# A mixer round's attention scores made in two halves, with the next round's first projection between them

## The reference

```python
h = rms_norm(x, g_mix[l])
z = h @ w_in[l]                                   # 1024 -> 6 x 512
u, gb, gc, q, k, v = jnp.split(z, splits, axis=-1)
y_conv = gb * short_conv(gc * u, conv_w[l])       # causal, width 3
q = rms_norm(q per head, g_q[l]) * (HEAD_DIM ** -0.5)
k = rms_norm(k per head, g_k[l])                  # 8 heads of 64
y_attn = dilated_mixture(q, k, v)                 # three dilated windows, mixed by exp(lse)
mix = concat(rms_norm(y_conv), rms_norm(y_attn))
x = x + mix @ w_out[l]
...                                               # gated feed-forward, then the second block
```

## Time and profile before

| what | value |
|---|---|
| median of 3 runs | 996.63 us |
| the profiled execution's own time | 998.33 us |
| its span from first to last instruction | 996.7 us |
| TensorE busy | 975.9 us (98%) |
| VectorE busy | 679.9 us (68%) |
| ScalarE busy | 415.0 us (42%) |
| mean granted TensorE clock, of full | 0.995 |
| rounds 0 to 3 of the mixer | about 39 to 190 us of the span |
| 512 KB weight load, median from issue to landing | 3.7 us |

### The profile page before, as it was taken

The page is one execution under the profiler, slowest core; times in us unless marked ns, Lnnn a source line. Parts: engine busy times, 40 slices in busy tenths (PEclk is TensorE's granted clock), DMA queues, the critical chain, the costliest instruction groups (busy, mean ns, idle before and its releaser), DMA issues.

```text
span 996.7 us, 14071 instructions
## 1 busy us (share of the span) xinstructions
PE 975.9 (98%) x4648; PEld 784.3 (79%) x4648; DVE 679.9 (68%) x1218; ACT 415.0 (42%) x671; POOL 171.7 (17%) x298
## 2 busy tenths in 40 slices
PE   6999999999999999999999999999999999989997
PEld 6876777677888888888888876888888887757886
DVE  6585786687676666655346668498978766865656
ACT  5455454634332323333221236945552326652343
POOL 3010101100000000197200000835760000000000
PEclk9999999999999999999999999999999999999999
DMA  6336757232562332334423223332243334542332
GB/s 216 92 92 201 203 165 197 55 97 85 170 188 85 105 104 86 91 109 136 145 90 105 85 75 109 100 85 69 64 106 88 101 100 89 149 116 69 107 89 85
DMA packets 146228, 112.22 MB, mean 113 GB/s; under 512 B 5100, under 2 KB 136428, under 8 KB 146188
## 3 DMA queue, kind: packets, MB, share of 16 engines
q1 hardware_dynamic: 138768, 85.83, 29.3%
q0 software_dynamic: 7184, 25.84, 9.5%
q10 hardware_dynamic: 236, 0.06, 0.0%
HBM read 99.65 MB, written 4.20 MB: 104 GB/s over the span
## 4 chain that ended last, share of the span: by engine, by line
PE 93%; DMA 2%; ACT 2%; DVE 2%; issue 0%; SPq 0%; DVEq 0%
PE bank L623 20%; PE bank L624 19%; PE bank L625 19%; PE bank L884 4%; PE bank L882 4%; PE bank L883 4%; PE bank L657 2%; PE bank L677 2%; PE bank L607 2%; PE bank L608 2%; PE bank L609 2%; PE bank L790 1%; PE bank L792 1%; PE bank L791 1%; PE bank L600 1%; DMA raw<-in_w_a_o_dram 1%
## 5 line engine op out<-in xcount | busy, mean ns | idle before, releaser
L623 PE MATMUL bank<-hH,wH 128*128 128x512 f32 x840 | 329.4, 392 | 0.1
L625 PE MATMUL bank<-hH,wL 128*128 128x512 f32 x840 | 327.0, 389 | 0.0
L624 PE MATMUL bank<-hL,wH 128*128 128x512 f32 x840 | 326.9, 389 | 0.0
L1582 DVE TENSOR_TENSOR wL<-raw,wH 128x1024 fp32r<-128x1024 f32 x155 | 196.3, 1267 | 155.4 <-ACT wH L1133 154.6
L1133 ACT ACTIVATE wH<-raw 128x1024 fp32r<-128x1024 f32 x155 | 164.0, 1058 | 268.1 <-PE bank L625 125.8
L623 PEld LDWEIGHTS bank<-hH,wH 128*128 128x128 f32 x840 | 157.7, 188 | 39.0 <-issue 6.2
L625 PEld LDWEIGHTS bank<-hH,wL 128*128 128x128 f32 x840 | 157.7, 188 | 33.1
L624 PEld LDWEIGHTS bank<-hL,wH 128*128 128x128 f32 x840 | 157.8, 188 | 31.7
L882 PE MATMUL bank<-aH,wH 128*128 (+1 forms) x160 | 62.2, 389 | 0.0
L883 PE MATMUL bank<-aL,wH 128*128 (+1 forms) x160 | 62.2, 389 | 0.0
L884 PE MATMUL bank<-aH,wL 128*128 (+1 forms) x160 | 62.2, 389 | 0.0
(11 more groups left out here) (479 smaller groups left out, 1486.0 us busy)
## 6 DMA issues: line engine op xcount, KB each, us to landing
raw<-in_w_in_dram SPq DMA_DIRECT2D x61, 512.0 KB, 3.7
mraw<-in_w_mod_dram POOLq DMA_DIRECT2D x24, 512.0 KB, 5.1
raw<-in_w_gate_dram SPq DMA_DIRECT2D x22, 512.0 KB, 3.8
raw<-in_w_up_dram SPq DMA_DIRECT2D x22, 512.0 KB, 3.7
raw<-in_w_down_dram SPq DMA_DIRECT2D x22, 512.0 KB, 3.3
raw<-in_w_out_dram SPq DMA_DIRECT2D x16, 512.0 KB, 3.7
pTd<-turned POOLq DMA_DIRECT2D x24, 320.0 KB, 6.3
x_tok<-in_x_dram SPq DMA_DIRECT2D x4, 512.0 KB, 5.5
```

The source lines that it names most:

```text
L623: mm(o, a, hH[:, k, :], start=(k == 0), stop=False)
L624: mm(o, a, hL[:, k, :], start=False, stop=False)
L625: ins = mm(o, b, hH[:, k, :], start=False, stop=(k == KD - 1))
L1582: TT(wL[s.par][:], raw[s.par][:], wH[s.par][:].bitcast(F32), SU).then_inc(lo_done, 1)
```

## The change

TensorE makes scores 0 to 3, then the projection Q', then scores 4 to 7, then K' and V'. VectorE reads scores 0 to 3, makes wL of K', reads scores 4 to 7, makes wL of V' and goes on with the rest, which is now not broken by a weight split. ScalarE takes exponentials 0 to 3, waits for TensorE to finish Q', makes wH of V', takes exponentials 4 to 7, and then copies Q' out. This holds for rounds 0 to 2; in the last round the scores stand in a row as before.

```diff
@@ tensor
-            def qkv(first, i):
-                for j in range(3):
+            def qkv(first, i, js=range(3)):
+                for j in js:
                     project(Slot(first, j, 6, i))
...
-                scores(i, qn, kn)
+                scores(i, qn, kn, range(2))
                 if not last:
-                    qkv(6, i)
+                    qkv(6, i, [0])
+                scores(i, qn, kn, range(2, TB))
+                if not last:
+                    qkv(6, i, range(1, 3))
@@ scalar
-            def qkv(first, i, a, between=None):
+            def qkv(first, i, a, between=None, values=True):
...
-                    split_hi(sl.next())
+                    if values or sq is sqk:
+                        split_hi(sl.next())
...
-            def softmax(a, order):
+            def softmax(a, order, between=None):
                 for u, (hh, b) in enumerate(order):
+                    if u == TB and between is not None:
+                        between()
...
-                softmax(i, in_turn)
+                def next_values():
+                    used(Slot(6, 0, 6, i))
+                    split_hi(Slot(6, 0, 6, i).next())
+                softmax(i, in_turn, None if last else next_values)
                 if not last:
-                    qkv(6, i, i + 1)
+                    qkv(6, i, i + 1, None, False)
@@ vector
-            def normalise(a, turning=None):
+            def normalise(a, turned_too=False):
...
-                    if turning is not None:
-                        if hh:
-                            turning()
+                    if turned_too:
                         dve.wait_ge(pn, a * 2 + (hh + 1))
                         for b in range(TB):
                             turn(hh, b)
...
-                if last:
-                    head_max(i, masks1, lambda: split_lo(gb.next()))
-                else:
-                    head_max(i, masks1)
-                    split_lo(gb.next())
+                head_max(i, masks1, lambda: split_lo(gb.next()))
+                if not last:
+                    split_lo(Slot(3, 3, 6, i).next())
                     if not first:
                         mod_rows(i - 1, range(4, 6))
...
-                normalise(i, None if last else lambda: split_lo(Slot(3, 3, 6, i).next()))
+                normalise(i, not last)
```

## The result

The changed kernel took 1009.98 us (median of 4 runs, 1008.31 to 1011.06), the kernel before 996.09 us beside it (4 runs). The ratio is 1.0137, 95% interval 1.0125 to 1.0149. The forecast was 1010.6 us, +14.0 us; measured are +13.9. The execution whose profile follows took 1011.06 us, its span 1009.5.

A forecast was written before the change was run, and what follows sets the result against it. TensorE's own instruction sequence was taken as the bound. Scores -1.2, U behind round 0 +1.7, GB +0.9, U behind rounds 1 and 2 +7.8, clock +4.8 make +14.0 us: 996.63 becomes 1010.6 us, range 1002 to 1013.5.

The forecast's parts named there:

- score time saved, rounds 0, 1, 2: TensorE, first score to head sums: two halves bring each round to 19.32 us, 1.2 us saved in all.
- wait for U behind round 0: TensorE waits 1.7 us for VectorE's wL of the next U, whose tail there has no first `mod_rows` pair.
- wait for GB in round 1: TensorE starts U without its earlier delay, so GB's load and split come 0.9 us too late; bounds 0 and 1.2.
- wait for U behind rounds 1 and 2: wL of U ready 16.0 us after the second half, wanted after 12.1: 3.9 us each, 7.8 together.
- lost by the clock: Granted clock halves in the 3.9 us gaps of rounds 1 and 2: 2.4 us each, 4.8 together; full-clock rival 0.25.
- What bounds it: TensorE's instruction sequence, busy 98% of the span, sets the end; any shift of its starts in a round goes through.
- The row's 1.8 us until the fall: Around 893 us TensorE had no matmul for 1.8 us at full clock before the fall; assumed for the new gaps.
- "in flight then": `w_mod` loads and moves of turned pieces were said to make GB's data take 12.0 us to land.
- The sentence from the Trainium skill: A 1 MB load runs at 341 GB/s, so GB's 512 KB need 1.5 us plus a fixed part; GB's wait 0.
- The rest of the span: The last round and all that follows were forecast only to shift, as before but later.

The follow-up runs named there:

- two rows in the idle time: Changed kernel with the first pair of `mod_rows` of rounds 1 and 2 moved into VectorE's idle time during Q'; 1000.53 us, 1.0056.
- the fitted order: Changed kernel with first `mod_rows` pair (rounds 1, 2) and `conv_low` during Q', U's split ahead of the second pair; 994.62 us, 0.9981.
- the two kernels with small moves: Changed kernel, U's split before second `mod_rows` pair, turned-probability moves cut to a tenth: 999.77 us; also two `w_mod` loads a round cut: 999.70 us.
- the moved splits alone: Changed kernel with TensorE's part undone (8 scores in a row, then Q', K', V'), VectorE's and ScalarE's new split places kept; 1012.53 us, 1.0173.
- TensorE's part alone: Kernel before with only TensorE's new order (scores 0 to 3, Q', scores 4 to 7, K', V'), VectorE and ScalarE as before; 1009.67 us, 1.0150.
- U's split earlier: Changed kernel with only the split of U moved ahead of the second pair of `mod_rows`; 1004.74 us, 1.0089.

## Why the prediction was right

Step by step, from the rows after against those before:

| step | forecast | measured |
|---|---|---|
| score time saved, rounds 0, 1, 2 | 0.18, 0.64, 0.41 | 19.50, 19.96, 19.73 less 19.33: 0.17, 0.63, 0.40 |
| wait for U behind round 0 | 1.7 | 1.60 |
| wait for GB in round 1 | 0.9 | 0.62 |
| wait for U behind rounds 1 and 2 | 3.9 each | 3.99, 4.08 |
| lost by the clock | 2.4 each | 2.8 and 1.6 |
| sum | +14.0 | +13.5 |

The shift of TensorE's timeline from the first score of round 0 (55.82 against 55.53) to GB of round 3 (184.24 against 170.27) is 13.97 - 0.29 = 13.7 us, so the steps account for all but 0.2.

That the forecast meets the measured +13.9 within 0.1 us is in part luck: the clock took 0.4 us more than forecast in one round and 0.8 less in the other, and the time of a single execution varies by more than that outside the rounds.

- **What bounds it** was right, and the experiment with two rows in the idle time shows it: 2.39 us out of the tail, 2.39 us off the wait.
- **The halves' saving** was right to 0.01 us a round, since the second block held an exact analogue. Taken alone it is what the kernel with the fitted order gains in the rounds: 1.23 us. The rest of its measured 1.7 to 1.9 us lies outside them and isn't explained; its profiled execution happened to have no fall of the clock at the earlier trace rows's place.
- **The clock.** It fell, as forecast, twice, and filling the gap kept it up. The size was taken from one row, and the two falls were not alike: from U's start to GB's are 138.66 - 122.43 = 16.23 us in round 2, where before it was 13.42, and 14.99 in round 3 (GB at 184.24), where before it was 13.43. The row's 1.8 us until the fall did not hold either: here it fell 3.2 us into the gap.
- **GB's load** was mis-sized, 0.9 for 0.62. Of the two kinds of transfers "in flight then" the experiments show the moves of turned pieces as those that count, and what the `w_mod` loads add is not separated. The forecast said "they shift along with VectorE, so I expect no relief", and that held for the changed kernel (11.8 us from U's split to the data, 12.0 before). Where an experiment moved U's split against them it was 11.9 us in one round and 14.1 in the next.
- The sentence from the Trainium skill, "DMA: Bandwidth & Descriptors", section "Measured", was rightly set aside for this place. It is given for loads issued from GpSimd, and these are issued from SyncE. With the moves cut, 512 KB took 3.6 us, which leaves 2.1 us for the fixed part beside the estimated 1.5.
- **The rest of the span.** From round 3 on the shift is 13.97 us (184.24 against 170.27). The whole span is longer by 12.8 only. The fall of the clock at the earlier trace rows's place lasts 3.4 us in the profile after and 6.8 in that of before. It varies from run to run: the same gap of 2.8 us stands there in all twelve profiles, and the clock fell in nine of them, for 3.4 or 6.8 us, and stayed at full in three (the fitted order and the two kernels with small moves).

## What to carry to other kernels

When work on the bounding engine is spread out so that it needn't wait for another engine, look at what that other engine does behind its last piece: it ends later by as much as the last piece was moved back, and everything in its order up to the next thing that the first engine needs moves with it. Here the 5.5 us of the projection Q' were taken out from between VectorE's last read and the next U, against 0.9 us of slack; the gain of 1.2 us was there when 3.6 us of VectorE's own work had gone into the hole that Q' made for it, and 2.4 us more behind U's split; 2.4 us in the hole alone still left waits of 1.6 and 1.7 us. Take such an edit apart at both ends, since two pins may hold the same chain.

## What the runs showed of the hardware

- Waits of 1.6 and 1.7 us between dense matmuls left the clock at full (the kernel with two rows in the idle time); each of the four profiled waits of 4.0 to 4.1 us brought it to half, for 3.4 or 6.8 us. Between them it went either way: it fell behind waits of 2.34 us (the moved splits alone, round 0) and 2.74 us (TensorE's part alone, rounds 1 and 2), and not behind 2.83 and 2.95 us (TensorE's part alone, round 0; U's split earlier, round 3). Behind one and the same gap of 2.8 us near 893 us it fell in nine profiles and not in three. 15 matmuls that compute nothing in the gap kept it at full.
- 512 KB loads from HBM landed in 11.2 us beside four 320 KB moves within SBUF, and in 3.6 us when these moves were cut to 16 KB, with 512 KB loads of `w_mod` issued among them both times (11.3 and 4.2 us).
- One more pair of changes between the 64-row and the 128-row form of matmuls took 0.2 us: Q' between the halves needs 104.55 - 98.89 = 5.66 us, where its matmuls at their spacing in the middle (22 in 5.00 us, 99.23 to 104.23) would need 5.46, so about 0.1 us goes at each end. Whether the change of form is the reason isn't shown: the first matmul behind a wait between two projections is longer by the same 0.1 us (117.16 to 117.50 in TensorE's part alone, 0.23 later on).
